# Ranking and placing tokens with one-pass F32R products in both layers of a hybrid decoder trunk

## The chip, the cores and the metric

The kernel runs on one core of a Trainium2 chip. The metric is the device time of one execution in microseconds (us), as the median of several runs. The engines are TensorE (PE, with PEld for its weight loads), VectorE (DVE), ScalarE (ACT), GpSimd (POOL) and SyncE (SP), which mostly issues DMAs.

## What is computed

Two layers over 1024 tokens of width 1024. Each layer has a token mixer (layer 0: mLSTM and gated linear attention; layer 1: sliding-window attention) and then a mixture of 32 experts, of which each token takes two in one group. The change is in the routing between the mixer and the experts. The reference:

```python
expert_ids = g_idx * EXPERTS_PER_GROUP + top_i          # two experts for each token
flat_e = expert_ids.reshape(-1)
order = jnp.argsort(flat_e)
e_sorted = flat_e[order]
counts = jnp.bincount(flat_e, length=N_EXPERTS)
padded = (counts + MOE_BLOCK - 1) // MOE_BLOCK * MOE_BLOCK
pad_end = jnp.cumsum(padded)
pad_start = pad_end - padded
start = jnp.cumsum(counts) - counts
dest = pad_start[e_sorted] + jnp.arange(n_assign, dtype=jnp.int32) - start[e_sorted]
tok_buf = jnp.zeros((n_pad,), jnp.int32).at[dest].set(flat_tok[order])
```

So each token needs its rank among the tokens of its expert, and each expert needs a table of the tokens that it serves.

## The kernel before

Tokens are held in T = 8 tiles of 128 (one token for each partition). The program of each engine is written out by hand, in order; an engine waits for another by semaphores, and nothing is reordered. The stages follow each other: layer 0's mixer (to about 573 us), its experts (to about 1130 us), layer 1's mixer (to about 1611 us), its experts, and a final sum and norm. An expert stage can't start before the table of its layer is complete, since its first gather reads it.

Routing goes tile by tile, woven into the mixer's last part:

- `take_logits` on DVE scales the router's product (L2044 in layer 0, L2877 in layer 1) and then calls `choose_experts` (L117 to L143), which finds the two experts of each token as one-hot rows `R.hot`, adds them to `R.both[:, t]` (L139), and adds the tiles before to a running sum that it keeps in the unused columns 4 to 35 of `logits` (L143). It ends with the semaphore `chosen`.
- `rank_tokens` on PE (L148, L149) makes two products into 32 columns of PSUM: the strict triangle `tri_strict` with `R.both`, and `ones` with the running sum. The sum of the two is each token's rank. Semaphore `ranked`.
- `mark_places` on DVE (L158 to L172) turns ranks into one-hot slots `R.slot_hot` (128 columns for each of two choices) and valued one-hot blocks `R.block_hot` (256 columns each). Semaphore `marked`.
- `enter_tokens` on PE (L178) makes two products, `slot_hot` with `block_hot`, into 256 columns. Semaphore `entered`. `take_entries` on DVE (L184, L185) adds them into the table `R.made`.
- After the last tile, `count` (L1376, L1377; in layer 1 L2564, L2565) makes two more products of `ones`, from which DVE reads the number of levels (L191 to L197); `make_tables` (L202 to L208) writes the tables, and POOL's first gather (L1111, in layer 1 L2381) waits for them.

On PE these calls stand between the mixer's own products: the output projection `project_out` (L1334, in layer 1 L2528), transposes (L1314, L1350, L2515, L2542), the router's product `route_product` (L1363, L2551). On DVE `take_logits(u)` waits for `ranked` and `entered` of earlier tiles and is followed in order by `residual` (L2017, in layer 1 L2857), which gives PE's `project_out` and `turn_rows` what they wait for. In layer 0 rank and enter are called from part 3 of `between` and, for the last tiles, from `after_mixing`; in layer 1 from its own `between`.

An FP32 product appears in the trace as two matmul records on PE, each with its own weight load; an F32R product appears as one. The heavy products of the kernel are F32R already, with each operand split in a high and a low part (names ending in `_hi` and `_lo`); the routing products are FP32. All the operands of the routing products are whole numbers.

Of the kernel before, what the change touches and what calls it, by code (L numbers as in the profile page):

```python
# [21 lines left out]
P = 128  # L22
# [67 lines left out]
class Routing:  # L90
# [11 lines left out]
    def scratch(self, x, y):  # L102

        self.slot_hot, self.valued = x[:, 0:256].rearrange("p (k n) -> p k n", k=2), x[:, 0:64].rearrange("p (k n) -> p k n", k=2)
        self.block_hot, self.work = x[:, 256:768].rearrange("p (k l n) -> p k l n", k=2, l=LEVELS), x[:, 256:320].rearrange("p (k n) -> p k n", k=2)
        self.none, self.table = x[:, 0:256], x[:, 256:512]
        self.both = x[:, 768:1024].rearrange("p (t e) -> p t e", t=8)
        self.made, self.masked, self.flags = y[:, 0:256], y[:, 256:288], y[:, 288:320]
        self.reached, self.level = y[:, 320:338].rearrange("p (k l) -> p k l", k=2), y[:, 338:354].rearrange("p (k l) -> p k l", k=2)
        self.below, self.slot, self.place = y[:, 354:356], y[:, 356:358], y[:, 358:360]  # L110


def choose_experts(v, dve, c, R, logits, t):
# [25 lines left out]
    v.tensor_tensor(R.both[:, t], R.hot[:, t % 2, 0], R.hot[:, t % 2, 1], ALU.add)  # L139
    if t == 0:  # L140
        last = v.memset(logits[:, 0, 4:36], 0.0)
    else:
        last = v.tensor_tensor(logits[:, t, 4:36], logits[:, t - 1, 4:36], R.both[:, t - 1], ALU.add)  # L143
# [3 lines left out]
def rank_tokens(mm, c, R, logits, t, ranks):  # L147
    mm(ranks, c["tri_strict"][:], R.both[:, t], start=True, stop=False)  # L148
    return mm(ranks, c["ones"][:], logits[:, t, 4:36], start=False, stop=True)  # L149
# [6 lines left out]
def mark_places(v, dve, c, R, t):  # L156
# [13 lines left out]
    v.tensor_scalar(R.late[:, :, t], R.block_hot[:, :, 0, N_EXPERTS - 1], 0.0, None, ALU.is_gt)  # L170
# [633 lines left out]
def make_constants(nc, mem, A):  # L804

    c = {}
    for name, shape, dt in (
        ("ident", [P, P], F32), ("ones", [P, P], F32), ("tri", [P, P], F32), ("tri_strict", [P, P], F32),
# [8 lines left out]
        c[name] = mem.sb(name, shape, dt)  # L817
    params = [("mix_gain0", A["mix_norm"][0], 8), ("mix_gain1", A["mix_norm"][1], 8), ("ml_gain", A["ml_head_norm"][0], 4), ("gla_gain", A["gla_head_norm"][0], 4),
# [22 lines left out]
def fill_patterns(nc, c, pool):  # L841
    for name, value in (("ident", 0.0), ("eps", EPS), ("ones", 1.0), ("tri", 1.0), ("tri_strict", 1.0), ("tri_gla", 1.0 / GLA_TAU),
                        ("causal_add", 0.0), ("last_row", 0.0), ("swa_add", 0.0)):
        nc.gpsimd.memset(c[name][:], value)
# [4 lines left out]
    for name, (pattern, step), op, fill in (  # L849
        ("ident", down, ALU.not_equal, 1.0), ("tri", up, ALU.is_ge, 0.0), ("tri_strict", up, ALU.is_gt, 0.0),  # L850
# [10 lines left out]
    pool.drain()  # L861
    nc.gpsimd.memset(c["tri_gla"][0:GLA_CHUNK, GLA_CHUNK:P], 0.0)
# [9 lines left out]
def layer0(nc, c, A, h, row_loads, const_loads, logits, router, gate_rows, u_rows, R, raw_ring, ring_ready, ahead):  # L872
# [6 lines left out]
    with ExitStack() as ctx:  # L879
# [22 lines left out]
        slots = mem.sb("slots", [P, SLOTS, 1024])  # L902
        scratch = mem.sb("scratch", [P, 1024])
# [19 lines left out]
        R.scratch(scratch[:], prep[:])  # L923
# [8 lines left out]
        root, scale, square = mem.sb("root", [P, T]), mem.sb("scale", [P, T]), mem.sb("square", [P, DV])  # L932
# [41 lines left out]
        with nc.Block() as block:  # L974
# [140 lines left out]
            def _(pe):  # L1115
# [259 lines left out]
                def count():  # L1375
                    mm(counted, c["ones"][:], R.both[:, T - 1], start=True, stop=False)  # L1376
                    mm(counted, c["ones"][:], logits[:, T - 1, 4:36], start=False, stop=True).then_inc(s["counted"], 1)  # L1377
# [769 lines left out]
def layer1(nc, keeper, before, c, A, h, weight, y_rows, logits, router, u_rows, R, raw_ring, ring_ready, S, ahead):  # L2147
# [9 lines left out]
    with ExitStack() as ctx:  # L2157
# [38 lines left out]
        R.scratch(work[6][:], turning[:, 0:384])  # L2196
# [187 lines left out]
        def tensor(pe):  # L2384
# [178 lines left out]
            def count():  # L2563
                nc.tensor.matmul(counted, c["ones"][:], R.both[:, T - 1], start=True, stop=False)  # L2564
                nc.tensor.matmul(counted, c["ones"][:], logits[:, T - 1, 4:36], start=False, stop=True).then_inc(s["counted"], 1)  # L2565
# [560 lines left out]
```

## Time and profile before

| | us |
|---|---|
| median of 3 runs | 2242.9 (2238.09 to 2243.27) |
| the profiled execution | 2239.22 |
| its span in the trace | 2237.5 |
| PE busy | 2110.7 (94%) |
| DVE busy | 1621.8 (72%) |
| ACT busy | 1344.3 (60%) |
| POOL busy | 275.5 (12%) |

The profiled execution took 1.7 us more than its span, and lies 3.7 us under the median of the runs. Matmuls are pipelined, so the duration of a PE record is longer than the distance from its start to the next one's: for what a product costs in a stream, the starts are to be compared. A number in square brackets at the end of a row of the timeline is idle time of the engine before that instruction, and the arrow tells what ended it.

### The profile page before, as it was taken

How to read it: one execution, taken by the hardware profiler on the slowest of the kernel's cores; microseconds unless marked ns; L12 is line 12 of the kernel's file. 1: busy time of each engine (PE TensorE's matmuls, PEld its weight loads, DVE VectorE, ACT ScalarE, POOL GpSimd, SP SyncE). 2: the span in 40 equal slices, each digit the busy share in tenths (PEclk: the TensorE clock that was granted, in tenths of full speed). 3: DMA queues.
4: the chain of work that ended last, by engine and by line, in shares of the span. 5: the costliest groups of instructions: out<-in, count | busy, mean ns of one | idle time of the engine just before them, and what ended most of it. 6: DMA issues, size and time to landing. Idle time of an engine off the chain costs nothing. (4 is left out here: it accounts for less than half of the span.)

```text
span 2237.5 us, 29989 instructions
## 1 busy us (share of the span) xinstructions
PE 2110.7 (94%) x10591; PEld 1724.6 (77%) x10591; DVE 1621.8 (72%) x1962; ACT 1344.3 (60%) x1668; POOL 275.5 (12%) x254
## 2 busy tenths in 40 slices
PE   7999998999599999999989988999599999999997
PEld 5778876778488888888868867887478888888884
DVE  4561333667698889888876276776599888888896
ACT  4332424454487787877772255563268887778874
POOL 1100000000111111111102310000011112222220
PEclk9999998999699999999999989999799999999999
DMA  4112312114599999999974020001289999999996
GB/s 131 38 52 82 82 57 76 57 57 170 178 378 387 389 389 382 380 381 379 389 297 144 1 85 1 20 20 76 84 313 390 377 382 384 388 387 390 382 377 246
DMA packets 122304, 513.24 MB, mean 229 GB/s; under 512 B 27229, under 2 KB 28330, under 8 KB 87402
## 3 DMA queue, kind: packets, MB, share of 16 engines
q1 hardware_dynamic: 102490, 474.09, 56.4%
q0 software_dynamic: 18576, 33.86, 4.0%
q10 hardware_dynamic: 1152, 4.19, 0.5%
q8 instruction: 48, 0.79, 0.1%
q14 instruction: 38, 0.31, 0.0%
HBM read 495.03 MB, written 50.86 MB: 244 GB/s over the span
## 5 line engine op out<-in xcount | busy, mean ns | idle before, releaser
L518 DVE TENSOR_TENSOR exp_w_lo<-ring_raw,first_w_hi 128x2048 fp32r<-128x2048 f32 x192 | 439.0, 2288 | 32.4 <-ACT first_w_hi L446 32.3
L518 DVE TENSOR_TENSOR exp_w_lo<-ring_raw,exp_w_hi 128x2048 fp32r<-128x2048 f32 x192 | 438.8, 2288 | 27.1 <-ACT exp_w_hi L446 26.7
L446 ACT ACTIVATE exp_w_hi<-ring_raw 128x2048 fp32r<-128x2048 f32 x192 | 368.0, 1919 | 63.3 <-PE exp_up_out L375 27.5
L446 ACT ACTIVATE first_w_hi<-ring_raw 128x2048 fp32r<-128x2048 f32 x188 | 360.9, 1919 | 70.7 <-PE exp_up_out L375 25.1
L375 PE MATMUL exp_gate_out<-exp_w_lo,exp_x_hi 128*128 128x512 f32 x512 | 202.0, 395 | 0.0
L375 PE MATMUL exp_y_out<-exp_w_lo,exp_hid_hi 128*128 128x512 f32 x512 | 201.5, 393 | 0.0
L375 PE MATMUL exp_up_out<-exp_w_lo,exp_x_hi 128*128 128x512 f32 x512 | 199.2, 389 | 0.0
L321 POOL DMA_INDIRECT y_rows<-exp_y,base_rows_y x63 | 82.3, 1306 | 931.9 <-ACT exp_y L466 916.3
L375 PE MATMUL exp_gate_out<-first_w_hi,exp_x_hi 128*128 128x512 f32 x272 | 111.2, 409 | 7.9 <-DVE exp_x_lo L546 6.9
L522 DVE TENSOR_TENSOR exp_x_lo<-exp_x_turned,exp_x_hi 128x1024 fp32r<-128x1024 f32 x62 | 75.9, 1225 | 52.9 <-ACT exp_x_hi L450 52.9
L375 PEld LDWEIGHTS exp_gate_out<-exp_w_lo,exp_x_hi 128*128 128x128 f32 x512 | 97.5, 190 | 19.4 <-issue 0.2
L375 PEld LDWEIGHTS exp_y_out<-exp_w_lo,exp_hid_hi 128*128 128x128 f32 x512 | 97.1, 190 | 19.2
L375 PEld LDWEIGHTS exp_up_out<-exp_w_lo,exp_x_hi 128*128 128x128 f32 x512 | 96.1, 188 | 19.9
L375 PE MATMUL exp_gate_out<-first_w_hi,exp_x_lo 128*128 128x512 f32 x272 | 108.2, 398 | 0.0
L332 POOL DMA_INDIRECT first_x_rows<-u_rows,base_rows_u x62 | 102.8, 1659 | 38.3 <-issue 17.8
L375 PE MATMUL exp_y_out<-exp_w_hi,exp_hid_hi 128*128 128x512 f32 x256 | 103.8, 405 | 3.8 <-DVE exp_hid_lo L533 3.8
L375 PE MATMUL exp_up_out<-exp_w_hi,exp_x_hi 128*128 128x512 f32 x272 | 106.0, 390 | 0.0
L375 PE MATMUL exp_up_out<-exp_w_hi,exp_x_lo 128*128 128x512 f32 x272 | 105.9, 389 | 0.0
L375 PE MATMUL exp_y_out<-first_w_hi,exp_hid_hi 128*128 128x512 f32 x256 | 102.3, 400 | 1.7 <-DVE exp_w_lo L518 1.7
L1163 PE MATMUL l_pair<-l0w_unit_hi,l0u_u_hi 128*128 128x512 f32 x256 | 103.5, 404 | 0.0
L375 PE MATMUL exp_y_out<-exp_w_hi,exp_hid_lo 128*128 128x512 f32 x256 | 101.7, 397 | 0.0
L1163 PE MATMUL l_pair<-l0w_unit_lo,l0u_u_hi 128*128 128x512 f32 x256 | 100.4, 392 | 0.0
(489 smaller groups left out, 4804.8 us busy)
## 6 DMA issues: line engine op xcount, KB each, us to landing
ring_raw<-in_expert_w_gate_dram SPq DMA_DIRECT2D x128, 1024.0 KB, 10.4
ring_raw<-in_expert_w_up_dram SPq DMA_DIRECT2D x128, 1024.0 KB, 10.9
ring_raw<-in_expert_w_down_dram SPq DMA_DIRECT2D x128, 1024.0 KB, 10.5
l0w_raw<-in_ab_w_in_dram SPq DMA_DIRECT2D x48, 256.0 KB, 2.8
ring_raw<-y_rows SPq DMA_DIRECT2D x8, 1024.0 KB, 4.9
finish_y<-y_rows SPq DMA_DIRECT2D x8, 1024.0 KB, 13.1
ring_raw<-in_swa_w_qkv_dram SPq DMA_DIRECT2D x5, 1024.0 KB, 9.0
base_h<-in_x_dram ACTq DMA_DIRECT2D x8, 512.0 KB, 6.8
```

The costliest lines, as they stand in the source:

```text
L321: pool.indirect_dma_start(y_rows, bass.IndirectOffsetOnAxis(ap=rows_y[:, e:e + 1], axis=0), y[e % 2][:], None, bounds_check=2047, oob_is_e ...
L332: pool.indirect_dma_start(x_rows[e % 2][:], None, u_rows, bass.IndirectOffsetOnAxis(ap=rows_u[:, e:e + 1], axis=0), bounds_check=1023, oob ...
L375: last = nc.tensor.matmul(out, x[:, k0 + k], w[:, k, cols], start=(first and k == 0 and t == 0), stop=(last_unit and k == K - 1 and t == 2))
L446: nc.scalar.activation(split[split_slot(unit)][0][:], raw[raw_slot(unit)][:], ACT.Copy).then_inc(hi_ready, 1)
L518: nc.vector.tensor_tensor(lo[:], raw[raw_slot(unit)][:], hi[:].bitcast(F32), ALU.subtract).then_inc(lo_ready[split_slot(unit)], 1)
L522: nc.vector.tensor_tensor(x_lo[:], x_turned[:], x_hi[:].bitcast(F32), ALU.subtract).then_inc(x_cols_s, 1)
L1163: last = mm(out, u[:, 2 * quarter + j, k], w[:, at], start=(k == 0 and n == 0), stop=(k == 7 and n == 2))
```

## The change

The routing products get F32R operands: `R.both`, the running sum (now `R.before`), `R.slot_hot` and `R.block_hot` are F32R tiles, and so are `tri_strict` and `ones_exact` (the same ones, seen as F32 by the other products that use them). DVE writes these tiles with the same instructions as before, into another type. The running sum moves out of `logits` into `R.before`; since the scratch space stays the same size, `both` and `before` hold four tiles each, reused in turn, in place of eight tiles of `both`. At tile 0 a `tensor_scalar` by zero takes the place of a `memset`. At the start, `tri_strict` is now the difference of `tri` and `ident`, made by one POOL `tensor_tensor`, in place of a memset and an affine select. The square scratch of layer 0 on ACT goes into `causal_add`, which is no longer read then. No instruction is moved to another place in an engine's order, and no semaphore is added or taken away.

```diff
-    def scratch(self, x, y):
-
-        self.slot_hot, self.valued = x[:, 0:256].rearrange("p (k n) -> p k n", k=2), x[:, 0:64].rearrange("p (k n) -> p k n", k=2)
-        self.block_hot, self.work = x[:, 256:768].rearrange("p (k l n) -> p k l n", k=2, l=LEVELS), x[:, 256:320].rearrange("p (k n) -> p k n", k=2)
+    def scratch(self, x, exact, y):
+
+        self.slot_hot, self.valued = exact[:, 0:256].rearrange("p (k n) -> p k n", k=2), x[:, 0:64].rearrange("p (k n) -> p k n", k=2)
+        self.block_hot, self.work = exact[:, 256:768].rearrange("p (k l n) -> p k l n", k=2, l=LEVELS), x[:, 256:320].rearrange("p (k n) -> p k n", k=2)
         self.none, self.table = x[:, 0:256], x[:, 256:512]
-        self.both = x[:, 768:1024].rearrange("p (t e) -> p t e", t=8)
+        self.both, self.before = (exact[:, at:at + 128].rearrange("p (t e) -> p t e", t=4) for at in (768, 896))
...
-    v.tensor_tensor(R.both[:, t], R.hot[:, t % 2, 0], R.hot[:, t % 2, 1], ALU.add)
+    v.tensor_tensor(R.both[:, t % 4], R.hot[:, t % 2, 0], R.hot[:, t % 2, 1], ALU.add)
     if t == 0:
-        last = v.memset(logits[:, 0, 4:36], 0.0)
+        last = v.tensor_scalar(R.before[:, 0], R.hot[:, 0, 0], 0.0, None, ALU.mult)
     else:
-        last = v.tensor_tensor(logits[:, t, 4:36], logits[:, t - 1, 4:36], R.both[:, t - 1], ALU.add)
+        last = v.tensor_tensor(R.before[:, t % 4], R.before[:, (t - 1) % 4].bitcast(F32), R.both[:, (t - 1) % 4].bitcast(F32), ALU.add)
...
 def rank_tokens(mm, c, R, logits, t, ranks):
-    mm(ranks, c["tri_strict"][:], R.both[:, t], start=True, stop=False)
-    return mm(ranks, c["ones"][:], logits[:, t, 4:36], start=False, stop=True)
+    mm(ranks, c["tri_strict"][:], R.both[:, t % 4], start=True, stop=False)
+    return mm(ranks, c["ones_exact"][:], R.before[:, t % 4], start=False, stop=True)
...
-        ("ident", [P, P], F32), ("ones", [P, P], F32), ("tri", [P, P], F32), ("tri_strict", [P, P], F32),
+        ("ident", [P, P], F32), ("tri", [P, P], F32), ("tri_strict", [P, P], F32R), ("ones_exact", [P, P], F32R),
...
+    c["ones"] = c["ones_exact"][:].bitcast(F32)
...
+    nc.gpsimd.tensor_tensor(c["tri_strict"][:], c["tri"][:], c["ident"][:], ALU.subtract)
...
+        with ExitStack() as under:
+            exact = Memory(nc, under, "l0e").sb("exact", [P, 1024], F32R)
         scratch = mem.sb("scratch", [P, 1024])
...
-        R.scratch(scratch[:], prep[:])
+        R.scratch(scratch[:], exact[:], prep[:])
...
-                    mm(counted, c["ones"][:], R.both[:, T - 1], start=True, stop=False)
-                    mm(counted, c["ones"][:], logits[:, T - 1, 4:36], start=False, stop=True).then_inc(s["counted"], 1)
+                    mm(counted, c["ones_exact"][:], R.both[:, (T - 1) % 4], start=True, stop=False)
+                    mm(counted, c["ones_exact"][:], R.before[:, (T - 1) % 4], start=False, stop=True).then_inc(s["counted"], 1)
...
-        R.scratch(work[6][:], turning[:, 0:384])
+        R.scratch(work[6][:], split_work[6][:], turning[:, 0:384])
```

The text of `enter_tokens` is unchanged; its operands change type. `exact` and `scratch` lie at the same place in memory.

## Rows read from the trace of the kernel before

**Rows 1.** The chain that ended last: one line of shares, and one expert's pieces.

```profile
PE 26%; DVE 1%; DMA 1%; ACT 0%; issue 0%; DVEq 0%; SPq 0%; ACTq 0%; POOLq 0%
...
1672.56 5.49 PE exp_y_out L375 x24
```

**Rows 2.** Busy time by stretch: PE, PEld, DVE, ACT, POOL; PE clock, DMA share, GB/s.

```profile
460.00:500.00 40.00, 39.46 (x258) 31.00 (x260) 24.36 (x76) 18.79 (x64) 0.00 (x0) 1.00 0.18 67
565.00:572.00 7.00, 3.67 (x12) 2.64 (x11) 3.91 (x19) 0.00 (x0) 0.00 (x0) 0.50 0.00 1
1640.00:2190.00 550.00, 548.34 (x2590) 454.76 (x2589) 495.06 (x290) 438.98 (x309) 109.24 (x58) 1.00 0.97 374
```

**Rows 3.** Timeline of layer 0, one middle tile: start, duration, engine, line.

```profile
452.72 0.39 PE L148 MATMUL l_pair<-l_scratch,base_tri_strict 128*128 128x32 f32 x2
...
452.95 0.39 PE L149 MATMUL l_pair<-base_logits,base_ones 128*128 128x32 f32 x2
...
453.17 1.11 PE L178 MATMUL l_pair<-l_scratch 128*128 128x256 f32 x4
...
454.12 1.05 PE L1285 MATMUL l_pair<-base_h,l_att 128*128 128x128 f32 x8
454.42 0.26 DVE L2044 SCALAR_TENSOR_TENSOR base_logits<-l_pair,l_scale,base_router_b 128x36 f32<-128x36 f32 x1 [0.66 <-PE l_pair L178]
```

**Rows 4.** Timeline, F32R products behind FP32 ones, weight loads too.

```profile
1537.33 0.19 PEld L2528 LDWEIGHTS l_wide<-l_w_hi,l1o_o_hi 128*128 128x128 f32 x1
1537.36 0.48 PE L2528 MATMUL l_wide<-l_w_hi,l1o_o_hi 128*128 128x512 f32 x1
1537.44 0.19 PEld L2528 LDWEIGHTS l_wide<-l_w_lo,l1o_o_hi 128*128 128x128 f32 x1
...
1537.67 0.40 PE L2528 MATMUL l_wide<-l_w_lo,l1o_o_hi 128*128 128x512 f32 x1
```

**Rows 5.** Who waited for whom on DVE in layer 0's mixing: total, times, longest.

```profile
DVE base_logits L2044 <- PE l_pair L178: 1.9, 4, 0.7
```

**Rows 6.** Timeline of layer 0 after the last tile was mixed.

```profile
515.04 0.50 PE L1334 MATMUL l_pair<-l_w_hi,l_o_hi 128*128 128x512 f32 x1 [0.82 <-DVE base_h L2017]
...
551.96 0.18 DVE L143 TENSOR_TENSOR base_logits<-base_logits,l_scratch 128x32 f32<-128x32 f32 x1
553.90 0.69 DVE L2017 TENSOR_TENSOR base_h<-l_pair,l_slots 128x512 f32<-128x512 f32 x1 [1.76 <-PE l_pair L1334]
```

**Rows 7.** Timeline of layer 0's last rank, last entry and table.

```profile
565.13 0.61 PE L149 MATMUL l_pair<-base_logits,base_ones 128*128 128x32 f32 x2
...
565.55 0.61 PE L1376 MATMUL l_pair<-l_scratch,base_ones 128*128 128x32 f32 x2
565.78 0.22 DVE L153 TENSOR_TENSOR l_scratch<-base_hot,l_pair 128x64 f32<-128x64 f32 x1 [0.82 <-PE l_pair L149]
...
568.94 2.08 PE L178 MATMUL l_pair<-l_scratch 128*128 128x256 f32 x4 [2.35 <-DVE l_scratch L172]
...
569.61 0.14 DVE L197 CAST base_levels<-base_choice 1x1 int32<-1x1 f32 x1
571.06 0.42 DVE L185 TENSOR_TENSOR l_prep<-l_prep,l_pair 128x256 f32<-128x256 f32 x1 [1.31 <-PE l_pair L178]
...
574.00 1.26 POOL L1111 DMA_INDIRECT first_x_rows<-u_rows,base_rows_u  x1 [11.22 <-DVE base_rows_u L208]
```

**Rows 8.** Timeline of layer 1, the tiles in which DVE waits for an entry.

```profile
1558.09 0.26 DVE L2877 SCALAR_TENSOR_TENSOR base_logits<-l_wide,l_scale,base_router_b 128x36 f32<-128x36 f32 x1 [3.21 <-PE l_wide L178]
...
1564.15 0.66 PE L2542 MATMUL l_wide<-base_ident,base_h 128*128 128x128 f32 x4 [2.75 <-DVE base_h L2857]
...
1586.66 1.99 PE L178 MATMUL l_wide<-l_work 128*128 128x256 f32 x4 [1.36 <-DVE l_work L172]
```

**Rows 9.** Timeline of layer 1's last entry.

```profile
1608.49 0.42 DVE L185 TENSOR_TENSOR l_turning<-l_turning,l_wide 128x256 f32<-128x256 f32 x1 [1.31 <-PE l_wide L178]
```

**Rows 10.** Timeline: a DVE write of an F32R tile of 512 columns.

```profile
536.28 0.68 DVE L2011 TENSOR_TENSOR l_o_lo<-l_pair,l_o_hi 128x512 fp32r<-128x512 f32 x1
```

More of the change, by code:

```diff
@@ L169, in mark_places @@
     dve.drain()
-    v.tensor_scalar(R.late[:, :, t], R.block_hot[:, :, 0, N_EXPERTS - 1], 0.0, None, ALU.is_gt)
+    v.tensor_scalar(R.late[:, :, t], R.block_hot[:, :, 0, N_EXPERTS - 1].bitcast(F32), 0.0, None, ALU.is_gt)
     for k in range(2):
@@ L841, in fill_patterns @@
 def fill_patterns(nc, c, pool):
-    for name, value in (("ident", 0.0), ("eps", EPS), ("ones", 1.0), ("tri", 1.0), ("tri_strict", 1.0), ("tri_gla", 1.0 / GLA_TAU),
+    for name, value in (("ident", 0.0), ("eps", EPS), ("ones_exact", 1.0), ("tri", 1.0), ("tri_gla", 1.0 / GLA_TAU),
                         ("causal_add", 0.0), ("last_row", 0.0), ("swa_add", 0.0)):
-        nc.gpsimd.memset(c[name][:], value)
+        nc.gpsimd.memset(c[name][:].bitcast(F32), value)
     nc.gpsimd.iota(c["iota"][:], pattern=[[1, P]], base=0, channel_multiplier=0, allow_small_or_imprecise_dtypes=True)
@@ L849, in fill_patterns @@
     for name, (pattern, step), op, fill in (
-        ("ident", down, ALU.not_equal, 1.0), ("tri", up, ALU.is_ge, 0.0), ("tri_strict", up, ALU.is_gt, 0.0),
+        ("ident", down, ALU.not_equal, 1.0), ("tri", up, ALU.is_ge, 0.0),
         ("tri_gla", up, ALU.is_ge, 0.0), ("causal_add", down, ALU.is_ge, NEG),
@@ L931, in layer0 @@
         state = mem.sb("state", [P, 2, DV + 1])
-        root, scale, square = mem.sb("root", [P, T]), mem.sb("scale", [P, T]), mem.sb("square", [P, DV])
+        root, scale, square = mem.sb("root", [P, T]), mem.sb("scale", [P, T]), c["causal_add"]
         pairs = [mem.ps(f"pair{j}", [P, 1024]) for j in range(4)]
@@ L2563, in count @@
             def count():
-                nc.tensor.matmul(counted, c["ones"][:], R.both[:, T - 1], start=True, stop=False)
-                nc.tensor.matmul(counted, c["ones"][:], logits[:, T - 1, 4:36], start=False, stop=True).then_inc(s["counted"], 1)
+                nc.tensor.matmul(counted, c["ones_exact"][:], R.both[:, (T - 1) % 4], start=True, stop=False)
+                nc.tensor.matmul(counted, c["ones_exact"][:], R.before[:, (T - 1) % 4], start=False, stop=True).then_inc(s["counted"], 1)
             def between(n, g, late):
```

## The prediction

> **What bounds the kernel now.** I read the chain of waits first: walked back from the end, 26% of the span lies on PE and 1% on each of DVE and DMA [rows 1]. The reader should see that every piece in the expert stage is PE work, and that 24 F32R products of 512 columns take 5.49 us there, 0.229 us each. Busy time by stretch says the same: from 1640 to 2190 us PE is busy for 548.34 of 550 us [rows 2]. So an expert stage has a fixed length, and whatever lets it start earlier moves the end by as much. Its start hangs on the routing table: POOL's first gather follows 11.22 us of idleness that ended with the table [rows 7]. The mixer ahead of it is PE's as well: 39.46 of 40 us from 460 to 500 [rows 2]. The routing products lie in that stream and in the serial tail behind it, where the granted clock is 0.50, the lower level of 1.2 GHz [rows 2].
>
> **The change part by part.** Each layer ranks 8 times (2 products each), enters 8 times (2 products each) and counts once (2 products). Each FP32 product is two records, each F32R product one.
>
> *Price of a rank at full clock.* L148 starts at 452.72, L149 at 452.95, L178 at 453.17 [rows 3]: 0.22 us a product, 0.11 us a record. The stream of 32 columns is short, so the weight load sets this. An F32R weight load takes about the same 0.11 us: two loads start at 1537.33 and 1537.44 [rows 4]. Hence 0.11 us a product, and a rank saves 0.22 us. *Price of an entry.* L178 to L1285 takes 0.95 us for four records of 256 columns [rows 3]. F32R: half of 0.229, so 0.115 us a product, plus about 0.07 us until the next operation, 0.30 us in all: 0.65 us saved. Both together save 0.87 us. *Switching.* The first F32R product behind FP32 work takes 0.31 us to the next start (1537.36 to 1537.67), against 0.23 [rows 4]: 0.10 us more, its weight load not being hidden. Where a tile's entry is followed by F32R products this was paid before; where it is followed by FP32 ones it is new, and the pair saves 0.77 us.
>
> No row shows an F32R product of under 512 columns. The bounds: below, the one-pass prices above; above, the FP32 prices themselves (nothing saved). I take the one-pass ones for the entry, since its 256 columns are nearest to the row; for the rank the nearer row is the weight load.
>
> Here a rule may be weighed. The Trainium skill, "TensorE: Matmul & The Clock Gate", section "Back-to-back issue gap", gives some 60 cycles to a product of at most 64 columns, with a floor of about 25 ns. The trace's 0.11 us a record [rows 3] does not show that gap, because here each record has weights of its own to load. By the page's figure alone each rank would save about 0.4 us, and the sum would be about 1 us larger.
>
> *Layer 0, mixing.* Here DVE sets what is gained. In `take_logits` it waits for the entry 4 times, 1.9 us in all, the longest 0.7 [rows 5] (0.66 at 454.42 [rows 3]). With entries earlier by 0.77 or more it starts earlier by those waits at most, then is bound by its own `normed_rows`; PE meets it again at `project_out`, where it already waits (0.82 at 515.04 [rows 6]). So 1.9 us. Behind the last mixed tile PE would save 2.39 us (two pairs, one lone entry); DVE has 1.76 us to give, its idleness before `residual` at 553.90, and that begins when its own chain ends at 552.14 (551.96 and 0.18) [rows 6]. So 1.76 us; 3.7 us together. Bounds: 2.5 if half of the DVE waits turn out to be filled by other work, 4.9 if PE alone decides.
>
> *Layer 0, tail.* At the lower clock a product of 32 columns takes 0.42 us (L149 at 565.13 to L1376 at 565.55), DVE waiting 0.82 us for it [rows 7]; with two products of half the price, 0.42 us are saved. The last entry takes 2.08 us; a record of 256 columns at 1.2 GHz is twice the 0.22 of full clock, 0.43, so four less two F32R ones at 0.21 save 1.28 us. DVE is then busy with the levels to 569.75 (L197), so L185 moves from 571.06 to about 569.85: 1.2 us [rows 7]. Together 1.6 us, nothing in the way up to the gather.
>
> *Layer 1.* DVE waits for PE before it takes logits, so PE's own savings count in full. The first rank, next to FP32 work: 0.12. Three tiles followed by FP32 products: 3 x 0.77 = 2.3. Two tiles where DVE waits 3.21 us for the entry and PE later 2.75 us for DVE's `residual` [rows 8], so that PE and DVE take turns and the whole 0.87 is on the path: 1.7. The entry at 1586.66 takes 1.99 us, mostly at the lower clock: 1.28 us if priced as above, 0.64 if the clock returns at the same moment and the saved time only lets more of the projection run slowly; I take 1.1. The tail repeats layer 0's: 0.42 and, from 1608.49 [rows 9], 1.2. The entry at 1596.60 and the rank before the 1.36 us wait for the marks [rows 8] are hidden: 0. Sum 6.9 us.
>
> *At no cost.* DVE writes the same elements in another type. The F32R write of 512 columns takes 0.68 us [rows 10], the F32 one 0.69 [rows 6], so no DVE step gets longer. The `tensor_scalar` for the `memset` is some 0.1 us, once a layer, before the first rank, which nobody waits for yet; were the cover gone, 0.2 us. `both` and `before` in four slots need no new wait: tile t - 4 was ranked long before. POOL at the start loses two short steps and gains one; 0.1 us either way.
>
> **Sum.** 3.7 + 1.6 + 6.9 = 12.2 us. Against the profiled execution, 2239.22 us (span 2237.5 and 1.7 around it), that is 2227.0. The median lies 3.7 us higher, so 2242.9 - 12.2 = 2230.7; I give **2230.5**. A measurement here tells about 0.3%, or 6.7 us, from no change.
>
> **The rivals.**
>
> *A, narrow F32R products keep the FP32 price, entries do not.* For it: no row shows 32 columns in F32R. Against: the weight load already covers the whole price. The ranks' 0.12 + 5 x 0.22 + 0.42 in layer 1 and 0.42 in layer 0 go: about 2 us. 2232.5.
>
> *B, the entries keep it too.* Then the change does not do what it says: within 1 us of before, 2242.5. Only the missing row speaks for it; the records at 512 columns speak against.
>
> *C, the savings are absorbed.* DVE is the partner that PE meets in each tile; if PE's time in layer 1 is met by DVE's chain as in layer 0, its mixing gives half (2 of 4.1), layer 0's about 2.5 of 3.7, and the low-clock entry 0.6: 8.4 us, so 2234.5. Against: in layer 1 DVE's waits for PE are 3 us long.
>
> *D, the clock falls earlier: slower.* PE gets shorter bursts, and its idle stretches between DVE's answers remain. The clock now is 1.00 from 460 to 500 and 0.50 in the tail, after PE had idled [rows 2]; in layer 1 it has gone down by 1586.66, after the waits that begin with the 2.75 us one [rows 8]. If the lower level reached back through the last two tiles (1564 to 1587, 23 us, of which PE works some 17), it would cost up to 17 us, leave 5 us of loss, and give 2248. It decides from about 12 us of PE work moved to the lower level. Against it: the stretch with waits of 2.75 us runs at full clock today, and each wait grows by 0.2 us at most. The Trainium skill has this as a rule ("TensorE: Matmul & The Clock Gate", "HAM oscillation"): idle gaps throttle the array to half its clock. By that rule a change that takes PE work out between waits is the dangerous kind; the trace agrees as far as the 0.50 behind idleness goes.
>
> **How the numbers follow.** Forecast (9 to 15 us of gain) 0.62; A 0.12; C 0.12; B 0.07; D 0.04; something unforeseen on either side 0.03. The forecast's own range: low 2242.9 - 15 = 2228, high 2234. The 3.7 us between profile and median, both of the same kernel, widen the whole: the low end goes to 2224, and the high end must take in A and C, to 2238.5. B and D are left out. Faster by over 0.3% (under 2236.2): the forecast, A and most of C, 0.82. Within: B and the rest of C, 0.13. Slower: D, 0.05.
>
> **What would show it.** L148, L149 and L178 with half their records (16 to 8, 32 to 16 in each layer, one a product); starts 0.11 us apart in a rank and 0.3 us from the first of an entry to the next operation. The waits of L2044 for L178 gone or short; `residual` of 553.90 with little idleness ahead; the last L178 about 0.8 us long and L185 right behind L197. Layer 0's gather some 5 us earlier, layer 1's some 12, the expert pieces still 5.49 us. The prediction is wrong if narrow records are as long as before, if DVE waits reappear elsewhere in the same amount, or if the clock of the mixers falls.

## The result and the profile after

| | before | after |
|---|---|---|
| median of 5 runs, us | 2239.06 (2237.26 to 2243.27) | 2226.28 (2218.15 to 2229.44) |
| the profiled execution, us | 2239.22 | 2229.44 |
| its span, us | 2237.5 | 2227.8 |
| its mean granted clock | 0.967 | 0.964 |

The ratio is that of the means (2240.1 and 2224.8), 0.9932, with a 95% interval of 0.9906 to 0.9958: 15.2 us less of 2239.06 (9.4 to 21.0), which is 2223.8 us. The two medians lie only 12.8 us apart. Forecast were 12.2 us less, and 2230.5 us. The profiled execution of the changed kernel is the slowest of its five; they had clocks of 0.964, 0.966, 0.967, 0.970 and 0.972, and the higher the clock, the shorter the time (2229.44, 2228.82, 2226.28, 2221.32, 2218.15). The repeats below come back to that.

From here on, lines from 826 on have 4 more than in the kernel before (L2044 is now L2048, and so on). First the page of the changed kernel: busy time, and the shares of the chain that ended last.

```profile
PE 2095.3 (94%) x10523; PEld 1713.7 (77%) x10523; DVE 1621.3 (73%) x1962; ACT 1342.5 (60%) x1668; POOL 246.2 (11%) x253
...
PE 27%; DVE 1%; ACT 0%; issue 0%; DVEq 0%; ACTq 0%
```

PE lost 15.4 us of busy time, more than the 9.7 us that the span lost; the chain is PE's as before [rows 1]. Busy time by stretch, the three of [rows 2], the tail's moved so that it starts 0.13 us ahead of the last rank's second product, as there (columns as there):

```profile
460.00:500.00 40.00, 39.04 (x260) 30.48 (x260) 25.06 (x78) 19.23 (x65) 0.00 (x0) 1.00 0.19 67
562.12:569.12 7.00, 1.73 (x6) 1.32 (x6) 5.03 (x22) 0.00 (x0) 0.00 (x0) 0.50 0.02 8
1640.00:2190.00 550.00, 546.42 (x2577) 453.45 (x2576) 487.82 (x279) 435.91 (x317) 81.33 (x59) 1.00 0.97 372
```

The tail is still at the lower level, and its PE work is halved: 6 records and 1.73 us in place of 12 and 3.67. Timeline of the middle tile of [rows 3]: start, duration, engine, line.

```profile
454.06 0.26 PE L148 MATMUL l_pair<-l0e_exact,base_tri_strict 128*128 128x32 f32 x1
...
454.17 0.26 PE L149 MATMUL l_pair<-l0e_exact,base_ones_exact 128*128 128x32 f32 x1
...
454.29 0.48 PE L178 MATMUL l_pair<-l0e_exact 128*128 128x256 f32 x2
...
454.61 1.05 PE L1289 MATMUL l_pair<-base_h,l_att 128*128 128x128 f32 x8
...
455.08 0.23 DVE L2048 SCALAR_TENSOR_TENSOR base_logits<-l_pair,l_scale,base_router_b 128x36 f32<-128x36 f32 x1
```

Half the records; the starts of a rank 0.11 us apart (0.22 before); the entry takes 0.32 us to the next operation (0.95 before). Together 0.55 us where it was 1.40, 0.85 us saved. L2048 waits for nothing now. For 256 columns an F32R product takes 0.115 us against 0.44 for an FP32 one, a quarter; for the 32 columns of a rank it is 0.11 against 0.22, only half. The Trainium skill, "FP8 and Floating Point Precision", section "TensorE Precision Notes", says that true FP32 takes four passes through the array; by this rule the trace agrees at 256 columns, though it shows them as two records of 0.22 us.

What DVE's waits become: PE's waits in layer 0's mixing, 420 to 520 us, before and then after (who waited for whom: total, times, longest).

```profile
PE l_pair L1334 <- DVE base_h L2017: 1.6, 4, 0.8
```

```profile
PE l_pair L1338 <- DVE base_h L2021: 2.6, 4, 1.3
```

PE is ready earlier and waits longer for the same DVE chain. The timeline behind the last mixed tile, and the tail, against [rows 6, 7]:

```profile
551.14 0.18 DVE L143 TENSOR_TENSOR l0e_exact<-l0e_exact 128x32 fp32r<-128x32 f32 x1
551.24 0.69 DVE L2021 TENSOR_TENSOR base_h<-l_pair,l_slots 128x512 f32<-128x512 f32 x1
...
562.25 0.38 PE L149 MATMUL l_pair<-l0e_exact,base_ones_exact 128*128 128x32 f32 x1
562.46 0.37 PE L1380 MATMUL l_pair<-l0e_exact,base_ones_exact 128*128 128x32 f32 x1
562.66 0.22 DVE L153 TENSOR_TENSOR l_scratch<-base_hot,l_pair 128x64 f32<-128x64 f32 x1 [0.37 <-PE l_pair L149]
...
565.83 0.79 PE L178 MATMUL l_pair<-l0e_exact 128*128 128x256 f32 x2 [2.78 <-DVE l0e_exact L172]
...
566.49 0.14 DVE L197 CAST base_levels<-base_choice 1x1 int32<-1x1 f32 x1
566.66 0.42 DVE L185 TENSOR_TENSOR l_prep<-l_prep,l_pair 128x256 f32<-128x256 f32 x1
```

`residual` (L2021) has no idle time ahead of it (1.76 us before), the wait for the rank is 0.37 (0.82), the last entry takes 0.79 us (2.08), and L185 stands right behind L197. Layer 1, against [rows 8, 9]:

```profile
1549.63 0.26 DVE L2881 SCALAR_TENSOR_TENSOR base_logits<-l_wide,l_scale,base_router_b 128x36 f32<-128x36 f32 x1 [2.35 <-PE l_wide L178]
...
1555.71 0.66 PE L2546 MATMUL l_wide<-base_ident,base_h 128*128 128x128 f32 x4 [2.79 <-DVE base_h L2861]
...
1579.02 0.79 PE L178 MATMUL l_wide<-l1s_work 128*128 128x256 f32 x2 [1.46 <-DVE l1s_work L172]
...
1599.15 0.42 DVE L185 TENSOR_TENSOR l_turning<-l_turning,l_wide 128x256 f32<-128x256 f32 x1
```

DVE's wait for the entry went from 3.21 to 2.35 us, by the 0.86 us of a rank and an entry; PE's wait for DVE stayed (2.75, now 2.79). The first gathers of the two expert stages start at 569.60 and 1602.00 us, 4.4 and 9.4 us earlier than before, where some 5 and 12 were forecast.

### The profile page after: what moved, and what is told of

It is laid out like the page before. It is cut to its first block and busy times, and to the rows that moved or that the text cites. A ratio compares the mean times of both kernels' runs of the same rounds, so it can differ in the third digit from the quotient of the medians.

```text
span 2227.8 us, 29852 instructions
## 1 busy us (share of the span) xinstructions
PE 2095.3 (94%) x10523; PEld 1713.7 (77%) x10523; DVE 1621.3 (73%) x1962; ACT 1342.5 (60%) x1668; POOL 246.2 (11%) x253
## 5 line engine op out<-in xcount | busy, mean ns | idle before, releaser
L321 POOL DMA_INDIRECT y_rows<-exp_y,base_rows_y x63 | 75.8, 1203 | 957.6 <-ACT exp_y L466 957.6
L1167 PE MATMUL l_pair<-l0w_unit_hi,l0u_u_lo 128*128 128x512 f32 x256 | 100.7, 393 | 0.0
```

The lines of the kernel that those rows point to most:

```text
L321: pool.indirect_dma_start(y_rows, bass.IndirectOffsetOnAxis(ap=rows_y[:, e:e + 1], axis=0), y[e % 2][:], None, bounds_check=2047, oob_is_e ...
L1167: last = mm(out, u[:, 2 * quarter + j, k], w[:, at], start=(k == 0 and n == 0), stop=(k == 7 and n == 2))
```

## The experiments

All were compared with the kernel before on the same chip. DVE executes 1962 instructions in the same order in each kernel, so the start of the same step can be compared across profiles. The table cuts each profiled execution at six of them: the last one of mixing before layer 0's routing (448.78 us in the kernel before), the last take of entries of layer 0 (571.06), a weight split in its experts (637.63) and one at their end (1129.40), a score of layer 1 behind its first rank (1457.80), its last take of entries (1608.49). The durations between them, worked out from the starts, in us. The stretch from 1129.40 to 1457.80 is layer 1's mixer up to its first rank, where the change does nothing but this rank; the last four rows are of kernels with added products, described below:

```
profile        routing, layer 0   ..637.63   experts   1129.40..1457.80   routing, layer 1
before                   122.28      66.58    491.76             328.40             150.69
before2                  122.27      66.53    491.76             327.76             150.45
e_layer0                 117.75      65.65    491.92             326.95             150.37
e_layer1                 122.25      66.66    491.77             327.68             145.16
e_rank                   121.84      66.78    491.76             327.73             150.48
e_enter                  117.44      65.78    491.76             322.19             150.20
after                    116.55      66.06    491.76             325.28             149.38
after2                   116.52      66.19    491.77             324.98             143.81
after3                   117.77      65.54    491.76             321.98             149.29
after4                   116.59      65.99    491.76             323.50             144.61
fill                     116.65      65.92    491.76             322.11             149.41
warm_before              121.22      67.41    491.77             325.28             153.73
warm                     118.33      67.18    491.76             327.71             144.93
warm2                    117.53      65.14    491.77             327.54             144.90
```

And the executions of the kernels without added products, with their mean granted clock (that of the five before in the first comparison is not on record, and they are left out). Within one kernel on one chip 0.001 of clock goes with 0.97 us (143 executions, those with added products among them, correlation -0.77). The last column uses this to compare each mean with the kernel before at an equal clock. It is an estimate, and it supposes that a difference of clock between two kernels costs what it costs within one, which no run shows; the warm runs below speak against it.

| kernel | executions | clock | mean us | less than before | at equal clock |
|---|---|---|---|---|---|
| before | 69 | 0.9657 | 2240.0 | | |
| changed (4 profiles above) | 21 | 0.9678 | 2225.5 | 14.5 | 12.5 |
| e_rank | 7 | 0.9689 | 2232.4 | 7.6 | 4.5 |
| e_enter | 5 | 0.9688 | 2227.1 | 12.9 | 9.9 |
| e_layer0 | 5 | 0.9684 | 2230.0 | 10.0 | 7.4 |
| e_layer1 | 11 | 0.9664 | 2232.2 | 7.8 | 7.1 |

**The changed kernel again (after2), and the kernel before against itself (before2).** No edit.

> The changed kernel again, for its steadiness and its clock. Theory 1 (the routing pieces themselves give 12 to 14 us, and the rest of the difference between single executions is the granted clock): the ratio to the kernel before stays at 0.993 to 0.9955, which is 10 to 15 us; executions of the changed kernel differ by 1 to 2 us for each 0.001 of mean granted clock; and the stretches of layer 1's mixer in which this profile's clock is at its lower level lie elsewhere than in the first profile (1526 to 1533 and 1557 to 1560 us there). Theory 2 (the change itself makes the clock fall in layer 1's mixer): the same stretches at the lower level again, and a ratio of 0.996 or above. Theory 3 (the change saves more than was priced): a ratio of 0.9925 or below, with no gain in layer 0's experts.

> The kernel before, as if it were a change of its own: ratio 1.000 within 0.001, for what the measurement gives where nothing differs. The executions so far have a mean granted clock of 0.9662 (11 of the kernel before) and 0.968 to 0.9695 (26 of the changed kernel and its variants). If that is chance of the session, the two halves here differ as much and this kernel's clock reaches 0.968; if the clock goes with the code, it is again 0.966 to 0.967, and its profile again shows lower-level stretches in layer 1's mixer near 1437 or behind 600 us that the profiles of the changed kernels lack.

after2: 2224.39 us, ratio 0.9933 (0.9920 to 0.9947), 15.0 us. before2: 1.0004 (0.9995 to 1.0013), so nothing differs where nothing is changed. The repeat gives the same size, 12 to 18 us, and is in the range expected for theory 1. The stretches at the lower level did not repeat in the second profile (routing of layer 1 143.81 us against 149.38), and before2 lacked both the one near 1437 and the one behind 600 us that the first profile of the kernel before had, and that were expected to return if the clock goes with the code. So single profiles differ by where the clock falls. The mean clock of before2, 0.9660, is again that of the kernel before, which was expected in that case too.

**The changed kernel a third and a fourth time (after3, after4).**

> The changed kernel a third time, beside more executions of the kernel before. Priced pieces alone (theory 1): 13.5 us less than before at an equal clock; if its mean clock is again 0.001 to 0.002 above that of the kernel before, at 1.1 us for each 0.001, the measured difference is 15 us (ratio 0.993); if the clocks are equal this time, 13 to 14 us (0.994).

> The changed kernel once more beside the one with layer 0's part alone. At an equal clock it is 12 to 13 us below the kernel before and 7 us below the kernel with layer 0's part alone; if its mean clock is again near 0.968, 14 to 15 us below before (ratio 0.9935), if it is at that of the kernel before, 12 to 13 us (ratio 0.9945).

0.9942 (0.9931 to 0.9954), 13.0 us, and 0.9938 (0.9925 to 0.9952), 13.9 us. The third gave the 13 us expected for equal clocks, although its clock was 0.9683; the fourth, at 0.9666, gave 13.9 us where 12 to 13 were expected. So the clock correction does not hold for five executions: by it, each set beside the kernel before on its own chip, the three repeats give 13.7, 10.0 and 13.9 us. The values at equal clock of the variants, which have 5 to 11 executions, are no surer than that. Of four profiles, two lose about 5 us in layer 1's routing (149.38 and 149.29) and two don't (143.81 and 144.61).

**Ranks and counts only (e_rank), entries only (e_enter).**

```diff
-        self.slot_hot, self.valued = exact[:, 0:256].rearrange("p (k n) -> p k n", k=2), x[:, 0:64].rearrange("p (k n) -> p k n", k=2)
-        self.block_hot, self.work = exact[:, 256:768].rearrange("p (k l n) -> p k l n", k=2, l=LEVELS), x[:, 256:320].rearrange("p (k n) -> p k n", k=2)
+        self.slot_hot, self.valued = x[:, 0:256].rearrange("p (k n) -> p k n", k=2), x[:, 0:64].rearrange("p (k n) -> p k n", k=2)
+        self.block_hot, self.work = x[:, 256:768].rearrange("p (k l n) -> p k l n", k=2, l=LEVELS), x[:, 256:320].rearrange("p (k n) -> p k n", k=2)
```

That was e_rank (one view of `block_hot` as F32 goes with it); in e_enter `both` and `before` lie in `x` instead, and

```diff
-    mm(ranks, c["tri_strict"][:], R.both[:, t % 4], start=True, stop=False)
-    return mm(ranks, c["ones_exact"][:], R.before[:, t % 4], start=False, stop=True)
+    mm(ranks, c["tri_strict"][:].bitcast(F32), R.both[:, t % 4], start=True, stop=False)
+    return mm(ranks, c["ones_exact"][:].bitcast(F32), R.before[:, t % 4], start=False, stop=True)
```

(and the counts likewise)

> Only the ranks and the counts in F32R, the entries left in FP32. If narrow products of 32 columns get cheaper like wide ones (the rank's two from 0.44 to 0.22 us): 0.2 us each for three tiles and 0.4 us in layer 0's mixing, 0.4 us in its tail, 1.5 us in layer 1, in all 2 to 4 us less than before, ratio 0.998 to 0.999. If a narrow product keeps its FP32 price (rival A of the prediction): nothing, ratio 1.000 within 0.0005, and the two records at L148 and L149 start 0.22 us apart as before.

> Only the entries in F32R, the ranks and counts left in FP32. As priced (0.65 us for each entry where PE's stream decides, 1.1 to 1.2 us for each last one): 4.8 us in layer 0, 5.5 us in layer 1, in all 10 us less than before, ratio 0.995 to 0.996; and DVE's wait for PE before L2048 in layer 0 is gone as in the changed kernel. If ranks and entries only pay together (what the rank saves is the part on the path): under 7 us, ratio 0.997 or above.

e_rank: 0.9965 (0.9954 to 0.9976), 7.8 us, where 2 to 4 were expected; the interval, 5.4 to 10.3, leaves them out. e_enter: 0.9940 (0.9926 to 0.9954), 13.4 us, where 10 were expected, just inside its interval. At equal clock, roughly, they give 4.5 and 9.9 us. As measured they add up to 21 us, more than the whole change gives. Timeline of e_rank, then of e_enter, the same tile:

```profile
448.00 0.26 PE L148 MATMUL l_pair<-l0e_exact,base_tri_strict 128*128 128x32 f32 x1
...
448.11 0.26 PE L149 MATMUL l_pair<-l0e_exact,base_ones_exact 128*128 128x32 f32 x1
...
448.22 1.11 PE L178 MATMUL l_pair<-l_scratch 128*128 128x256 f32 x4
449.17 1.05 PE L1289 MATMUL l_pair<-base_h,l_att 128*128 128x128 f32 x8
449.47 0.26 DVE L2048 SCALAR_TENSOR_TENSOR base_logits<-l_pair,l_scale,base_router_b 128x36 f32<-128x36 f32 x1 [0.44 <-PE l_pair L178]
```

```profile
453.06 0.39 PE L148 MATMUL l_pair<-l_scratch,base_tri_strict 128*128 128x32 f32 x2
...
453.28 0.39 PE L149 MATMUL l_pair<-l_scratch,base_ones_exact 128*128 128x32 f32 x2
453.51 0.49 PE L178 MATMUL l_pair<-l0e_exact 128*128 128x256 f32 x2
453.83 1.05 PE L1289 MATMUL l_pair<-base_h,l_att 128*128 128x128 f32 x8
454.13 0.26 DVE L2048 SCALAR_TENSOR_TENSOR base_logits<-l_pair,l_scale,base_router_b 128x36 f32<-128x36 f32 x1
```

By the starts each piece has its forecast price alone: a rank 0.22 us in place of 0.44, an entry 0.32 in place of 0.95. With the rank alone DVE still waits for the entry, 0.44 in place of 0.66 us, so all of its 0.22 us counts. Rival A is out. In layer 1's routing stage, though, neither profile is shorter than before (150.48 and 150.20 us): both have the clock at its lower level there for a while, e_enter near 1522 and 1553, e_rank near 1558.

**Layer 1 only (e_layer1), layer 0 only (e_layer0).**

The edit of e_layer1; in e_layer0 it is layer 1's `scratch` that gets `work[6]` twice and `seen` as F32.

```diff
-    mm(ranks, c["tri_strict"][:], R.both[:, t % 4], start=True, stop=False)
+    mm(ranks, R.seen(c["tri_strict"]), R.both[:, t % 4], start=True, stop=False)
...
-        R.scratch(scratch[:], exact[:], prep[:])
+        R.scratch(scratch[:], scratch[:], prep[:])
+        R.seen = lambda x: x[:].bitcast(F32)
...
         R.scratch(work[6][:], split_work[6][:], turning[:, 0:384])
+        R.seen = lambda x: x[:]
```

> F32R routing products in layer 1 only; layer 0's ranks, counts and entries in FP32 as before. By the prediction's sum 6.9 us less than before, by the steps seen in the traces (0.86 us for each middle tile, 0.8 to 1.2 for the later ones, 1.7 in the tail) 8 us, at an equal clock; layer 0's steps at L2048 and at the tail are gone. If the excess of the changed kernel over the forecast came from layer 0, this one saves under 6 us.

> F32R routing products in layer 0 only; layer 1's ranks, counts and entries in FP32 as before. By the prediction's sum 5.3 us less than before at an equal clock. The changed kernel's executions had a mean clock of 0.968 to 0.9685, those of the kernel before 0.9657, those of the kernel with layer 1 alone 0.9664. If the higher clock goes with layer 0's part, this kernel has 0.968 or more and measures 7 to 8 us less than before (ratio 0.9965 to 0.997); if it is chance or needs both parts, 0.966 and 5 to 6 us (ratio 0.9973 to 0.9978).

e_layer1: 0.9968 (0.9959 to 0.9977), 7.2 us; in its profile layer 0's routing takes 122.25 us as before, layer 1's 5.3 to 5.5 less, after a loss of 1.3 us at 1558, where the clock fell for a while. Forecast was 6.9. e_layer0: 0.9952 (0.9939 to 0.9966), 10.8 us, and 7.4 at equal clock; the forecast 5.3 lies below its interval (7.6 to 13.7), and so do the 7 to 8 us expected for the higher clock, but for the last tenths. Its profile shows 4.5 us less in layer 0's routing and 0.9 less up to 637.63, 5.4 together, and layer 1's routing as before. Its clock, 0.9684, is near the changed kernel's mean; with layer 1 alone the clock is 0.9664. But the changed kernel beside it on the same chip (after4) had 0.9666, and the kernel before 0.9658. The parts, 7.2 and 10.8, add up to more than the whole.

**More PE work behind the entries (fill).** Three tiles of each layer; the repeated products write what is then written again.

```diff
-                        for head in range(4):
+                        for head in ((0, 0) if t >= 5 else ()) + (0, 1, 2, 3):
...
+                        if n >= 5 and g == 3 and (i, b) == (0, 0):
+                            for _ in range(8):
+                                nc.tensor.matmul(out[:, local * HEAD_DIM:(local + 1) * HEAD_DIM], p_cols,
+                                                 vals[:, n + b - 1, (g // 2) * HEAD_DIM:(g // 2 + 1) * HEAD_DIM], start=True, stop=True)
```

> The changed kernel with products repeated on PE right behind the entries of three tiles of each layer: in layer 0 two more FP32 products of 128 columns for each tile (0.4 to 0.5 us), in layer 1 eight more of 64 columns (0.8 to 0.9 us), each of which is written over by the same product as in the changed kernel. If in layer 0's mixing PE waits for DVE anyway (PE's waits of 0.39, 0.38 and 1.33 us before L1338), layer 0's end moves by at most 0.4 us, and those waits shrink by as much as was added; in layer 1, where PE decides, all of 3 x 0.86 = 2.6 us comes back, in all 2.5 to 3.5 us over the changed kernel. If PE decides in both layers: 1.3 + 2.6 = 3.9 us or more. If DVE decides in both: under 1 us, and then the 8 us gained in layer 1 don't come from PE's stream.

Ratio 0.9936 (0.9921 to 0.9952), 2225.53 us, 1.1 us over after2 beside it, where 2.5 to 3.5 were expected, and no more than the changed kernel's mean: the whole time does not tell, and the profile has to. (The stretch ahead of layer 1's routing, ahead of any added product of layer 1, took 322.11 us against 324.98, which hides what was given back behind it.) The added work in layer 1 was mispriced: these products are FP32, 16 records and 1.73 us a tile (from 1465.21 to 1466.94 in the first), not 0.86. Layer 0 is clear. Its 0.45 us a tile are in the profile (L1289 x12), and its routing takes 116.65 us against 116.55. PE's waits there:

```profile
PE l_pair L1338 <- DVE base_h L2021: 1.4, 2, 0.9
```

2.6 us in four waits became 1.4 in two: PE's waits took up what was added. In layer 1 the starts show 0.97, 0.98 and 1.54 us given back of 1.73 each, 3.5 of 5.2; the 0.73 and 0.77 us that PE waits before L2546 in two of these tiles took up the rest. So DVE decides in layer 0's mixing, as forecast; in layer 1 PE decides, except in the shadow of DVE's `residual`, which lies behind the place of the filler and not behind the entry.

**PE kept busy in the tails (warm, warm_before, warm2).** Products nobody reads, into a free bank, in PE's idle time: before the last rank, between counts and last entry, behind it, and before the first expert's gate products.

```diff
+def keep_busy(nc, c, bank, n):
+    for _ in range(n):
+        nc.tensor.matmul(bank, c["ones_exact"][:], bc(c["ones_exact"][:], 1, 4), start=True, stop=True)
...
                     enter(a)
+                    keep_busy(nc, c, AB, 26)
                     rank(b)
                     count()
+                    keep_busy(nc, c, AB, 10)
                     enter(b)
+                    keep_busy(nc, c, AB, 42)
```

> The changed kernel with products nobody reads (ones by ones, 512 columns, 0.23 us each) in PE's idle time around the routing tails of both layers: behind the last entry but one, between the count and the last entry, behind the last entry, and between the first expert's transposes and its gate products. If the granted clock at its lower level behind the tails (about 31 us in each layer) comes from PE's idle time there, it stays at 1.00: the last ranks, counts and the last entry cost 0.7 us less in each layer, the transposes 0.9, the first 11 (layer 0) and 14 (layer 1) gate products 0.2 each, in all 8 us less than the changed kernel, ratio to before 0.989 to 0.990. If the level falls anyway, or falls later instead, the time stays within 2 us of the changed kernel's or gets longer by the products that don't fit into the idle time.

> The kernel before with the same products nobody reads in the same places. The worth of the change with the clock held up in the tails is the difference of this to the changed kernel with them: by theory 1 12 us (the tails' ranks, counts and entries save half as much at the full clock, 1.6 us less over both layers, and what the clock of the tails adds to the difference is gone); if the change worked mainly through the clock, under 8 us.

> The changed kernel with fewer of the products nobody reads: 18, 7 and 28 (layer 0) or 27 (layer 1) in place of 26, 10, 42 and 21, 9, 40, and the same 13 behind the transposes. In the first form the last rank of layer 0 came 1.0 us late and the first gather's end with the move to the next stage 1.7 to 1.9 us late, because PE was still at work. If those waits were all that ate the gain of the full clock (2.3 us in layer 0, 2.9 us in layer 1 behind the transposes), this form is 4 to 5 us faster than the changed kernel, ratio to before 0.991 to 0.992. If the clock falls again once PE is idle for 3 us before the transposes, it is equal to the changed kernel within 1 us.

warm: 0.9946 (0.9933 to 0.9959), 12.1 us, no gain over the changed kernel where 8 us were expected. warm_before: 0.9992 (0.9983 to 1.0001). warm2: 0.9940 (0.9927 to 0.9954), 13.4 us, 2225.63 us: equal to the changed kernel, where 4 to 5 us less were expected if only the waits had eaten the gain. The clock did rise, to 0.977, 0.978 and 0.975, and the work behind the tails did get shorter. Busy time by stretch, first stage of experts, of after2 and then of warm2 (PE clock is the third number from the end):

```profile
575.00:600.00 25.00, 19.33 (x78) 15.38 (x79) 18.56 (x23) 14.49 (x14) 5.42 (x4) 0.79 0.72 250
```

```profile
575.00:600.00 25.00, 21.94 (x90) 17.59 (x91) 19.95 (x25) 16.38 (x15) 6.06 (x4) 0.86 0.73 251
```

By the starts, the first expert gains 2.25 us in warm2 over after2 (from 575.21 to 595.22); of this 1.4 is lost again by 619, and the last rank's operands come 1.4 us later (L143 at 561.08 against 559.64). In warm the filler itself came in the way: 42 products of 0.229 us behind the entry of 565.40 keep PE in layer 0's part until about 575.3, and the next stage's first gather starts at 577.75, against 574.37 in after2. Nor is that all: in the stretch ahead of layer 1's routing, which the filler does not touch, both profiles took as long as the kernel before (327.71 and 327.54 us), 3.7 us more than the four of the changed kernel in the mean. No version beats the changed kernel. What the pair says of the change: with the clock held up in the tails, it is worth 10.1 us in the means (2238.2 less 2228.1), where 12 was expected, and under 8 if the clock were its main effect. With 5 and 11 executions this difference is sure to about 3 us (an estimate from their spread), so it speaks for the routing pieces and does not alone rule out 8.

## Why the prediction was right or wrong

**The mechanism was right.** The price of a rank (0.22 us saved) and of an entry (0.65 forecast, 0.63 measured by 0.95 to 0.32) hold. *Layer 0* was forecast as 3.7 + 1.6 = 5.3 us with DVE as the one that decides. Its routing got 5.7 us shorter in three profiles of the changed kernel and 4.5 in one. By steps of the first profile: L2048 gains 0.64, 0.72, 0.36 and 0.29 us, 2.0 where 1.9 stood; `residual` 1.82 where 1.76 stood; the tail 0.45 and 1.28 where 0.4 and 1.2 stood. The filler shows that DVE decides in the mixing. Where 4.5 us appear, the clock fell sooner behind the last projections (at 552.4 us in after3, at 556.6 in the first profile) and the router's last products ran slowly, which gave back 1.2 us.

**Layer 1, 6.9 us,** is 7.2 in the experiment with this layer alone (5.2 to 9.2 by its interval). Inside, the 0.77 for a pair in front of FP32 products was too small: three steps of 0.86 us, no price of switching was seen. The entry for which 1.28 or 0.64 was possible, and 1.1 was taken, gave 1.07 and lost 0.42 right behind it (e_layer1 against before2), so 0.65: the lower alternative. Two small readings in the prediction do not come out of its rows: the switch costs 0.08 us there (0.31 less 0.23), not 0.10, and half of the DVE waits in layer 0's mixing would leave 2.7 us (0.95 and 1.76), not 2.5. For that mixing's upper bound of 4.9 us no working is shown.

**The sum, 12.2 us,** is 12.5 at equal clock, and the agreement is in part luck. Take the mean of the four profiles of the changed kernel and that of the two of the kernel before: layer 0's routing and what follows up to 637.63 give 6.0 us, where 5.3 were forecast, but layer 1's routing gives only 3.8 of 6.9 (1.2 and 1.3 in two profiles, 6.0 and 6.8 in the others), and 4.1 us come from the stretch ahead of it, in which the change does nothing but one rank, worth 0.25 us.

The step that failed is the last of the sum, "The median lies 3.7 us higher, so 2242.9 - 12.2 = 2230.7", together with the range built on it. Of the 5 us between 2230.5 and the mean of 2225.5, 2.9 are this base: 2242.9 is the median of 3, and 69 executions of the kernel before have a mean of 2240.0, close to the 2239.22 that the prediction had and left aside. The range took the 3.7 us in, "the low end goes to 2224"; but that is 15 us under 2239.22, so with the base at its real place no room was left for a gain above 15. The first comparison gave 15.2, which is 2223.8, and seven of the 21 executions of the changed kernel lie under 2224.

The other 2.3 us (14.5 measured less 12.2) are a gain for which the sum has no term. "The 3.7 us between profile and median, both of the same kernel" took the granted clock for noise common to both kernels and put a difference between them at nothing. There is one: 0.9678 against 0.9657. At what the clock costs within one kernel this would be 2 us. That it is the cause is not shown: with the products nobody reads the mean clock rose by 0.0126 in the kernel before for 1.8 us, and by 0.0092 in the changed kernel for no gain at all. Where the 2.3 us come from stays open.

**Rival D** was given 0.04 as a loss over all. Its mechanism is there in small. Busy time by stretch at the same work in layer 1, behind the waits of [rows 8]: before, after, e_layer1, e_layer0.

```profile
1560.00:1565.00 5.00, 2.25 (x13) 1.62 (x12) 3.67 (x18) 0.15 (x1) 0.00 (x0) 1.00 0.00 2
```

```profile
1550.00:1555.00 5.00, 2.92 (x13) 2.07 (x11) 3.48 (x19) 0.00 (x0) 0.00 (x0) 1.00 0.02 6
1555.00:1560.00 5.00, 4.29 (x14) 3.55 (x15) 2.74 (x13) 0.60 (x1) 0.00 (x0) 0.67 0.00 0
```

```profile
1555.00:1560.00 5.00, 2.22 (x9) 1.72 (x8) 3.85 (x19) 0.60 (x1) 0.00 (x0) 0.75 0.01 2
```

```profile
1555.00:1560.00 5.00, 2.72 (x14) 2.34 (x15) 3.93 (x19) 0.60 (x1) 0.00 (x0) 1.00 0.01 2
```

In 8 of the 10 profiles whose layer 1 has F32R ranks or entries the clock falls for a short while here, between 1552 and 1558 us; in none of the 4 with FP32 ones. It costs 1.3 to 1.6 us. Together with a second one near 1522 to 1530 it took 5 us of the 7 in two profiles of the changed kernel; but such a second one stands in the profile of warm_before too (near 1532; 153.73 us for this stage), so that one does not need F32R. The Trainium skill's rule that idle gaps throttle the array ("TensorE: Matmul & The Clock Gate", "HAM oscillation") speaks for the direction, but the trace does not show the gap as the cause here: PE's longest wait ahead of this place is 2.75 us in the kernel before and 2.79 in the changed one, and after2 and after4 have it too (2.78 us) and the clock stays up.

And yet the mean clock over all executions is higher. In the profiles the stretch from 1129.40 to 1457.80 differs most. In it the clock is at its lower level for 27 to 44 us in all, and over the 14 profiles the longer it is, the longer the stretch takes, from 322.0 to 328.4 us (correlation 0.93). The changed kernel's four took 322 to 325.3 us, the two of the kernel before 328. But e_rank, e_layer1, warm and warm2, all with F32R products in layer 1, took 327.5 to 327.7 us, and warm_before, with FP32 ones, 325.28: it is not shown that F32R shortens it. Why the clock moves there, in code that was not touched, is open. That it goes with layer 0's part is a guess from 0.9684 for this part alone against 0.9664 for layer 1's; 5 executions with a spread of 0.001 are thin, and after4, which has both parts, had 0.9666 on the same chip. Also open is why the two layers alone sum to 18 us, with intervals of about 2 and 3 us on them, and ranks and entries alone to 21.

**Rivals B and C** are out: records and starts halved, and in layer 1 the gain was not met by DVE: by C this layer would give 4.2 us (2, 0.6 and 1.6), and e_layer1's interval is 5.2 to 9.2. Nothing at no cost turned out to cost: DVE's F32R writes take as long as FP32 ones (0.18 us at 551.14, 0.18 before at 551.96 [rows 6]), the wait at L2048 is gone, and the experts' stretch takes 491.76 or 491.77 us in all four profiles of the changed kernel and both of the kernel before.

## What to carry to other kernels

Where the values are whole numbers small enough to be exact, the small FP32 products of a routing step are worth a look: by starts in the trace an FP32 one of 256 columns costs four times an F32R one, one of 32 columns twice, and some stand in serial tails. Price each from the partner that waits: in one layer here the partner's slack was the gain, in the other PE's whole saving. Before a sum is set against a median, look how the clock differs between executions; here, within one kernel, 0.001 of mean clock went with 1 us, and the changed kernel's mean was 0.002 higher. And take the time before from more than three executions: the median of 3 was 2.9 us off the mean of 69.

## What the runs showed that was not expected

- One profile is one draw of where the clock falls. Between two executions of the same kernel the stage of layer 1's routing took 143.81 and 149.29 us, and that of the experts 491.76 and 491.77.
- Keeping PE busy in the tails raised the mean clock from 0.968 to 0.975 and 0.977 and gained nothing in time: what was won behind the tail was waited away or lost later. Here a higher mean clock by itself was worth nothing.
- A DVE `tensor_scalar` that takes 0.24 us took 2.49 us at 557.67 in the changed kernel while POOL ran a `tensor_tensor` of 1024 columns (557.27, 2.86 us). It lies in the serial tail of layer 0, and in the kernel before as well (2.48 us at 560.34, POOL's at 559.93). In after3 another DVE instruction met it: L125, a `tensor_tensor` of 32 columns that takes 0.19 us elsewhere, took 2.78 us at 555.97 with POOL's at 555.85. That POOL is the cause is read from this meeting and was not tested by moving it.
